# Experts stage: a third buffer for the indirectly loaded up weights, and another order of the plain weight loads

## The reference, cut to what matters

```python
for e in range(N_EXPERTS):                      # 32, D_EXPERT = 256
    he = jax.nn.silu(t @ w1e[e]) * (t @ w3e[e]) # up products, w1e and w3e side by side: 1024 x 512
    out = out + cw[:, e:e + 1] * (he @ w2e[e])  # down product, 256 x 1024; cw is zero but for two experts
```

## Time and profile before

| what | before |
|---|---|
| median of 3 runs | 2633.89 us (2633.48 to 2634.75) |
| the profiled execution | 2638.19 us, span 2636.3 us |
| TensorE busy | 2485.2 us, 94% |
| mean granted clock | 0.984 |
| the expert steps | 2277 to 2590 us of the span |
| q1, q0 | 313.98 MB, 18.19 MB |

### The profile page before, as it was taken

How to read it: one execution, slowest core, us unless ns; L and a number is a source line. 1 busy time by engine, 2 the same in 40 slices (tenths; PEclk the granted TensorE clock), 3 DMA queues, 4 the chain that set the end, 5 groups by cost and what they waited for, 6 DMA issues and landing times. The chain is left out here.

```text
span 2636.3 us, 38832 instructions
## 1 busy us (share of the span) xinstructions
PE 2485.2 (94%) x15328; PEld 1851.8 (70%) x15328; DVE 1150.0 (44%) x1584; ACT 950.7 (36%) x1384; POOL 999.5 (38%) x495
## 2 busy tenths in 40 slices
PE   8999999999999999999999999999898999599996
PEld 5777787788877688778778877676686776333334
DVE  5543523566553623432456654434754414311113
ACT  5543532544433434252444442344323214111112
POOL 5231522444377422351444447642224422323330
PEclk9999999999999999999999999999999999799998
DMA  3111322222266210321232236321001215699993
GB/s 134 72 49 54 107 96 80 97 90 89 75 231 214 81 65 32 112 96 64 80 112 95 90 112 235 137 97 71 2 4 50 81 63 208 232 391 346 364 352 106
DMA packets 76282, 333.88 MB, mean 127 GB/s; under 512 B 17114, under 2 KB 21210, under 8 KB 51802
## 3 DMA queue, kind: packets, MB, share of 16 engines
q1 hardware_dynamic: 62336, 313.98, 33.5%
q0 software_dynamic: 13824, 18.19, 2.0%
HBM read 372.67 MB, written 16.78 MB: 148 GB/s over the span
## 5 line engine op out<-in xcount | busy, mean ns | idle before, releaser
L227 PE MATMUL bank<-dense_s_hi,dense_w_hi 128*128 128x512 f32 x672 | 267.1, 397 | 12.8 <-POOL dense_w_lo L715 6.9
L228 PE MATMUL bank<-dense_s_lo,dense_w_hi 128*128 128x512 f32 x672 | 261.8, 390 | 0.0
L229 PE MATMUL bank<-dense_s_hi,dense_w_lo 128*128 128x512 f32 x672 | 261.8, 390 | 0.0
L715 POOL TENSOR_TENSOR dense_w_lo<-weights,dense_w_hi 128x1024 fp32r<-128x1024 f32 x77 | 199.6, 2592 | 94.4 <-ACT dense_w_hi L684 90.4
L1596 DVE TENSOR_TENSOR hidden<-up_y 128x512 f32 x44 | 158.1, 3594 | 64.6 <-ACT up_y L1560 64.0
L229 PE MATMUL bank<-xn_r,weights_r 128*128 128x512 f32 x448 | 176.0, 393 | 0.0
L2057 DVE SCALAR_TENSOR_TENSOR xn<-mix,xn 128x1024 f32<-128x1024 f32 x64 | 114.2, 1785 | 114.5 <-DMA mix<-in_modulation 108.6
L227 PEld LDWEIGHTS bank<-dense_s_hi,dense_w_hi 128*128 128x128 f32 x672 | 126.0, 188 | 53.6 <-POOL dense_w_lo L715 15.3
L1573 POOL TENSOR_TENSOR up_w_lo<-weights,up_w_hi 128x2048 fp32r<-128x2048 f32 x22 | 101.5, 4615 | 126.9 <-ACT up_w_hi L1548 126.9
L229 PEld LDWEIGHTS bank<-dense_s_hi,dense_w_lo 128*128 128x128 f32 x672 | 126.1, 188 | 26.7
L227 PE MATMUL bank<-xn_r,mix_r 128*128 128x512 f32 x352 | 140.7, 400 | 2.8 <-POOL up_xn_lo_r L363 2.6
(11 more groups left out here) (758 smaller groups left out, 6253.9 us busy)
## 6 DMA issues: line engine op xcount, KB each, us to landing
weights<-in_w_up SPq DMA_DIRECT2D x44, 1024.0 KB, 4.8
mix<-in_modulation SPq DMA_DIRECT2D x64, 512.0 KB, 5.0
weights<-in_w_xattn SPq DMA_DIRECT2D x24, 1024.0 KB, 5.0
weights<-in_experts_up SPq DMA_DIRECT2D x24, 1024.0 KB, 11.9
moe_weights<-in_experts_up SPq DMA_DIRECT2D x24, 1024.0 KB, 14.1
weights<-in_w_down SPq DMA_DIRECT2D x44, 512.0 KB, 3.8
rec_rkv<-in_experts_up SPq DMA_DIRECT2D x16, 1024.0 KB, 10.5
weights<-in_w_attn SPq DMA_DIRECT2D x8, 1536.0 KB, 6.4
```

The lines of the kernel that those rows point to most:

```text
L227: nc.tensor.matmul(out, left.hi, right.hi, start=first, stop=False)
L228: nc.tensor.matmul(out, left.hi, right.lo, start=False, stop=False)
L229: return nc.tensor.matmul(out, left.lo, right.hi, start=False, stop=last)
L715: nc.gpsimd.tensor_tensor(w[b].lo[:, :], units.rows(b, 0, D, 0, D), w[b].hi[:, :], ALU.subtract).then_inc(w_split, 1)
```

## The change

There are three buffers for the halves of the more tiles' up weights instead of two, used in turn: half s of tile o takes buffer (2o + s) mod 3, with a semaphore for each buffer. Half 0 of tile o now waits for the end of the up products of tile o-2 (the last user of its buffer), and half 1 for the middle of those of tile o-1. POOL clears the third buffer too. SP's loop now goes over the steps: in round n it asks for the up weights that replace those of step n, then for the down weights that replace those of step n-1.

```diff
-        more_up_ready, more_down_ready = ([sem(f"more_{what}_ready{i}") for i in range(2)] for what in ("up", "down"))
+        more_up_ready, more_down_ready = ([sem(f"more_{what}_ready{i}") for i in range(n)] for what, n in (("up", 3), ("down", 2)))
...
-        more_ups = [sb(f"more_up{s}", [P, moe.UP])[:, :] for s in range(2)]
+        more_ups = [sb(f"more_up{s}", [P, moe.UP])[:, :] for s in range(3)]
...
-            for e in range(4, EXPERTS):
-                sp.wait_ge(up_done, main_step[e - 4] + 1)
-                moe.load_up(sp, e)
-                sp.wait_ge(down_done, 2 * main_step[e - 4] + 2)
-                moe.load_down(sp, e)
+            for n in range(main_step[EXPERTS - 5] + 2):
+                for e in range(4, EXPERTS):
+                    if main_step[e - 4] == n:
+                        sp.wait_ge(up_done, n + 1)
+                        moe.load_up(sp, e)
+                for e in range(4, EXPERTS):
+                    if main_step[e - 4] == n - 1:
+                        sp.wait_ge(down_done, 2 * (n - 1) + 2)
+                        moe.load_down(sp, e)
...
                 for s in range(2):
-                    if o > 0:
-                        pool.wait_ge((up_half_done, up_done)[s], more_step[o - 1] + 1)
-                    nc.gpsimd.indirect_dma_start(out=more_ups[s], out_offset=None, in_=moe.w_up,
+                    if s == 0 and o > 1:
+                        pool.wait_ge(up_done, more_step[o - 2] + 1)
+                    if s == 1 and o > 0:
+                        pool.wait_ge(up_half_done, more_step[o - 1] + 1)
+                    nc.gpsimd.indirect_dma_start(out=more_ups[(2 * o + s) % 3], out_offset=None, in_=moe.w_up,
...
-            pool.wait_ge(cleared, 2)
+            pool.wait_ge(cleared, len(more_ups))
...
-                        weights.append(more_ups)
+                        weights.append([more_ups[(2 * more + s) % 3] for s in range(2)])
                 for k in range(KT):
                     if k % 4 == 0 and more is not None:
-                        pe.wait_ge(more_up_ready[k // 4], 16 * more + 16)
+                        q = 2 * more + k // 4
+                        pe.wait_ge(more_up_ready[q % 3], 16 * (q // 3) + 16)
```

More of the change, by code:

```diff
@@ L3236, in load_more_up @@
                 for s in range(2):
-                    if o > 0:
-                        pool.wait_ge((up_half_done, up_done)[s], more_step[o - 1] + 1)
-                    nc.gpsimd.indirect_dma_start(out=more_ups[s], out_offset=None, in_=moe.w_up,
+                    if s == 0 and o > 1:
[3 more added lines that the diff above has]
+                    nc.gpsimd.indirect_dma_start(out=more_ups[(2 * o + s) % 3], out_offset=None, in_=moe.w_up,
                                                  in_offset=bass.IndirectOffsetOnAxis(ap=moe.more_up[:, s, o:o + 1], axis=0),
-                                                 bounds_check=2 * EXPERTS * P - 1, oob_is_err=False).then_inc(more_up_ready[s], 16)
+                                                 bounds_check=2 * EXPERTS * P - 1, oob_is_err=False).then_inc(more_up_ready[(2 * o + s) % 3], 16)
             def load_more_down(o):
```

## The result

| | before | after |
|---|---|---|
| median | 2634.02 us (2633.48 to 2634.75, 4 runs) | 2655.02 us (2653.32 to 2659.13, 4 runs) |
| profiled execution, span | 2638.19, 2636.3 | 2653.32, 2651.5 |
| mean granted clock | 0.984 | 0.981 |

The ratio of the runs is 1.0084 (95%: 1.0072 to 1.0096): 0.84% slower, 21.0 us by the medians, 2 us from the forecast. The two profiled executions differ by 15.1 us only. The rest lies in executions that no profile shows.

The account below looks back on a forecast made before the run. TensorE (busy 294.7 of 313 us) and the DMA engines (0.88) were both taken as near their limit. -8.0 + 3.5 + 15.0 + 6.3 + 6.4 = +23.2 us gave 2657 us on the median, range 2630 to 2672.

Parts of the forecast that it names:

- the landing: Half 0 before steps 5 to 20: lands 11 to 13 us after its request, instead of 9.3 or 9.8.
- waits before steps 3, 4 and their clock: Start: earlier requests for experts 5 and 6 remove 0.92 + 4.39 + 2.66 = 8.0 us.
- step 2: Its really loaded 2 MB on q0 now share with expert 5's 2 MB: 3.5 us lost, between 0 and 6.1.
- step 5, with clock: Gets the wait of the others once step 4's hold-up goes: 4.7 + 1.6 = 6.3 us.
- five waits, steps 8 to 20: Half 0 lands 3.0 us later (bounds 0 and 4.9) before each step as q1 stays busy: 15.0 us.
- their clock: Up products behind the five waits run partly at half clock: 5 x 1.6 less 1.6 already there, 6.4 us.
- The buffers, 0: Three buffers: half 0 goes out at the same instant after the scatter; worth 0, up to a 1 us win.
- The start, -8.0 and +3.5: First steps: 8.0 us of waits and clock go at steps 3 and 4, 3.5 us lost in step 2.
- the 413 that were left: Of q0's 576 packets, those not through at 2380: took 2.7 us at 152 a us, now 7.6 at 54.
- the empty stretch: q1's hole while q0's packets were served; forecast to move before t = 19, leaving q1 busy through q0's four transfers.
- Rival (b): Start's gain comes, five waits stay, step 5 gets 1.7 us: 2627.6 us; something besides q1 delays half 0; chance 0.12.
- Rival (a): The named waits go away; a landing 2 us sooner removes the five waits and one clock loss: 2616; chance 0.05.

Follow-up runs that it names:

- buf_only: The changed kernel with SP's old loop, so only the three buffers differ from the kernel before: 2637.13 us, ratio 1.0006.
- start_only: The kernel before with SP's new order only for the requests up to expert 7: 2636.84 us, ratio 1.0003.
- one_held: The changed kernel with one up-weight request in each group of three steps held back 4.6 us, behind down weights: 2643.93 us, ratio 1.0024.
- hole_filled: The kernel before with one up-weight request in each group of three steps moved 4.6 us earlier: 2668.68 us, ratio 1.0125.
- before_gather: The changed kernel with half 0 asked for ahead of the round's gather, not behind it: 2644.67 us, ratio 1.0021.
- kept_busy: The changed kernel with 16 idle TensorE products before the wait for half 0 in steps 5, 8 and so on: 2655.09 us, ratio 1.0057.

## Why the prediction was right, step by step

The direction and the time were right, and so was the mechanism: q0's transfers are slowed while q1 has work. The sizes of two terms were not, and one piece of the working, the landing, does not follow from the count. The terms of the sum, against the profile after:

| term | forecast | measured |
|---|---|---|
| waits before steps 3, 4 and their clock | -8.0 | -8.0 |
| step 2 | +3.5 | +3.5, and 0.2 of lengthening |
| step 5, with clock | +6.3 | +8.9 (6.09 + 2.84) |
| five waits, steps 8 to 20 | +15.0 | +7.2 (15.8 - 8.7) |
| their clock | +6.4 | +4.8 (2.96 + 1.69 + 1.70 - 1.54) |
| sum | +23.2 | +16.6 (the stretch of the steps grew by 16); +21.0 by the medians |

Not in the table: step 0's products took 9.89 us instead of 8.41, and step 1's 7.09 instead of 8.78, which all but cancel.

**The buffers, 0.** Right: `buf_only` is at 1.0006, and half 0 goes out at the same distance from the scatter.

**The start, -8.0 and +3.5.** Each was right, but the account was cut in the wrong place. Step 5's wait belongs in good part to the start: `start_only` shows that the 8.0 come back as waits of q0 before steps 2 and 5, 2.74 us of it before step 5. I had step 5 as an ordinary member of the later series. It is the longest of all, 6.09 us, and even with the request held back (`one_held`) it stays at 5.68. Two causes are likely for what lies above 2.74. The up weights of experts 8 and 9 are asked for sooner in both of these kernels, and not in `start_only`. And three of the earlier more tiles are really loaded. No run changed either by itself, so this is argued and not shown.

**The five waits, +3.0 each.** This term was mis-sized: +1.4 each. The mechanism holds (`one_held`, `hole_filled`). I took q0's rate beside q1 to be 54 packets a us for nearly all of the 413 that were left, and gave little for the 1 MB of down weights in 4 KB packets. The three stretches of queue rows above show q0 at 60, 125 and 46 a us. The middle one, taken by single microseconds, has two parts. From 2384 to 2385 the small packets passed, and the queues again made equal counts, 102 of q0 and 101 of q1. In the next two q0 made 120 and 153, and q1 only 73 and 57, its share down to 78% and 84%: q1 still leaves gaps, and q0 moves on in them. Why q1 leaves them is not shown. From 2387 to 2389 the counts are equal again, 56 and 56, then 58 and 57. So the empty stretch did not vanish as I had it, but shrank. Half 0 landed 8.9, 11.1, 8.4, 10.5 and 10.1 us after its request, not 11 to 13, and of the six waits only one (4.43) lies within the 4 to 5.5 named.

The count does not give the landing either. My 2.7 us for the 413 packets end at 2382.7, but half 0 landed at 2385.8. In the changed kernel 576 packets are through at about 2387.4 and it landed at 2389.8. These 3.1 and 2.4 us stood in no term. The packets of half 1, asked for behind it, pass in that time: before the change 694 of the 720 packets of all five transfers were through by 2385. So it is not shown that the transfers are done strictly one behind the other, and what fills the last 2 to 3 us stays open. Rival (b) had named such a remainder. (Rival (a) was counted too well: a landing 2 us sooner leaves 0.63 and 1.13 us of the two longest waits.)

**The clock.** Three of the five products lengthened, by 1.7 to 3.0 us, where I had given each 1.6. Steps 8 and 14 waited 2.31 and 1.79 us and lost nothing.

**The page's rule.** The Trainium skill ("DMA: Bandwidth & Descriptors", "Queues, rings and completion order") has a DMA engine drain a whole packet of some 9 to 17 descriptors before it turns to another queue. Each indirect transfer has 9 of the profile's packets on an engine, so both readings give a wait that grows with the number of transfers ahead, and `before_gather` (2.9 us for one) agrees with both: 144 / 54 = 2.7 by the count, 2.4 by an estimate from the page. The runs don't tell them apart.

The errors of the terms have opposite signs: two that were too large (7.8 and 1.6) and one too small (2.6). The medians moved 6 us more than the profiles, so part of the nearness to 2657 is luck.

## What to carry to other kernels

Before moving a bulk request earlier, look at what small, urgent transfers run in the stretch that it will fill: a queue's idle time may be what lets them through. An indirect transfer that moves one row and skips 127 still puts 144 packets in the queue; count the packets ahead of an urgent one, and not the bytes alone. And a new buffer pays only if the request that it frees is also moved in the issuing engine's program: look whether the row before the transfer says "issue" or names the engine that it waits for.

## What the runs showed that I had not expected

One request of 2 MB asked for 4.6 us sooner in each group of three steps, in a kernel whose DMA engines are busy for 0.88 of the time, cost 34 us (2634.84 to 2668.68). Some 8 of them are step 6, held up by main weights.

An idle stretch of TensorE is not followed by the half clock according to its length alone: 3.1 us (step 17, before) and 2.31 us (step 8, after) cost nothing, while 1.89 us in `buf_only` was followed by up products of 8.79 us. The same 2.31 us before step 5 in `kept_busy` was followed by 8.78.
